# Causal masks of a differential attention moved off TensorE, with narrow diagonal tiles paired and the projections paced by each tile's surplus of ScalarE time

## The reference, cut to what matters

```python
xn = rmsnorm(x, norm_mix_g); u = xn @ w_in          # b, c, v_a | q, k, v | gates
y_a = short_gated_conv(b_g, c_g, v_a, conv_w) @ w_a_out
# four heads, each with two softmax maps of width 64 (c = 0, 1), values of width 128
s = einsum('bqhcd,bkhcd->bhcqk', q, k) * 64**-0.5
s = where(dist >= 0, s - slope[h] * dist, -inf)     # dist = qpos - kpos
p = softmax(s); a = p[:, :, 0] - lam * p[:, :, 1]
o = rmsnorm(einsum('bhqk,bkhv->bqhv', a, v), subln_g) * (1 - lam_init)
x = x + (g_a * y_a + g_b * (o @ w_b_out)) @ w_o     # sigmoid gates
x = x + square(relu(rmsnorm(x, norm_mlp_g) @ w_mlp_in)) @ w_mlp_out
out = rmsnorm(x, norm_final_g)                      # x: 4 x 4096 x 1024 float32
```

## Time and profile before

| | before |
|---|---|
| runs, us | 1248.42, 1382.58, 1246.85 (median 1248.42) |
| profiled execution, us | 1246.68 |
| its span, slowest core (3) | 1245.1 |
| spans of the eight cores | 1238.4 to 1245.1 |
| TensorE matmul busy | 1190.1 (96%) |
| VectorE busy | 596.2 (48%) |
| ScalarE busy | 643.8 (52%) |
| GpSimd busy | 62.1 (5%) |

### The profile page before, as it was taken

The page is one execution under the profiler, slowest core; times in us unless marked ns, Lnnn a source line. Parts: engine busy times, 40 slices in busy tenths (PEclk is TensorE's granted clock), DMA queues, the critical chain, the costliest instruction groups (busy, mean ns, idle before and its releaser), DMA issues.

```text
span 1245.1 us, 27807 instructions; the slowest of 8 cores (1238.4 to 1245.1 us)
## 1 busy us (share of the span) xinstructions
PE 1190.1 (96%) x7688; PEld 591.8 (48%) x7688; DVE 596.2 (48%) x964; ACT 643.8 (52%) x1010; POOL 62.1 (5%) x78
## 2 busy tenths in 40 slices
PE   3799999999999999999999999999999999999994
PEld 1355455555555555554444444444444444444442
DVE  3566426353434434323346436427364554637765
ACT  3455347888877897777755774330302112030066
POOL 0000001000000000000000000000000000000024
PEclk9899999999999999999999999999999999999998
DMA  8567310000100000018740507010321303031024
GB/s 169 154 179 185 75 35 2 2 3 2 36 2 3 2 2 3 2 36 150 186 104 1 135 2 131 23 34 1 68 32 38 68 1 68 1 69 21 14 86 186
DMA packets 17192, 71.97 MB, mean 58 GB/s; under 512 B 2416, under 2 KB 2672, under 8 KB 14608
## 3 DMA queue, kind: packets, MB, share of 16 engines
q0 software_dynamic: 6768, 35.65, 16.8%
q1 hardware_dynamic: 10272, 34.55, 8.0%
HBM read 97.46 MB, written 8.39 MB: 85 GB/s over the span
## 4 chain that ended last, share of the span: by engine, by line
PE 91%; DMA 2%; DVE 2%; ACT 2%; issue 1%; POOL 0%; DVEq 0%; ACTq 0%; POOLq 0%; SPq 0%
PE ps_all L294 71%; PE ps_all L291 11%; PE ps_all L296 7%; PE ps_all L315 1%; DMA big<-xs 1%; DMA big<-w_in 1%; ACT big L302 1%; DVE big L609 0%; ACT big L575 0%; DVE big L1089 0%; DVE big L318 0%; PE ps_all L641 0%; DVE big L1071 0%; ACT big L1084 0%; ACT big L304 0%
## 5 line engine op out<-in xcount | busy, mean ns | idle before, releaser
L294 PE MATMUL ps_all<-big 128*128 128x512 bf16 (+2 forms) x4416 | 950.0, 369 | 18.1 <-DVE big L318 14.9
L294 PEld LDWEIGHTS ps_all<-big 128*128 128x128 bf16 x4416 | 406.2, 98 | 500.7 <-issue 54.6
L575 ACT ACTIVATE big<-ps_all,big 128x512 bf16<-128x512 f32 (+3 forms) x384 | 313.8, 866 | 68.3 <-PE ps_all L296 26.9
L1059 ACT ACTIVATE big<-ps_all 128x512 bf16<-128x512 f32 x128 | 76.4, 597 | 336.6 <-PE ps_all L294 336.2
L1071 DVE TENSOR_TENSOR big<-ps_all,big 128x512 f32<-128x512 f32 x256 | 176.3, 691 | 39.2 <-PE ps_all L294 35.4
L291 PE MATMUL ps_all<-big 128*128 128x129 bf16 x2176 | 165.5, 221 | 3.2 <-DVE big L609 1.1
L291 PEld LDWEIGHTS ps_all<-big 128*128 128x128 bf16 x2176 | 129.3, 98 | 43.1 <-issue 35.7
L1060 DVE TENSOR_TENSOR big<-big 128x512 bf16<-128x512 bf16 x128 | 54.6, 426 | 165.9 <-ACT big L1059 165.9
L296 PE MATMUL ps_all<-big 64*128 64x512 bf16 (+3 forms) x640 | 114.6, 354 | 2.3 <-ACT big L575 1.1
L302 ACT ACTIVATE big<-big 128x1024 bf16<-128x1024 f32 (+1 forms) x65 | 68.6, 1055 | 60.0 <-PE ps_all L294 25.5
L318 DVE TENSOR_TENSOR big<-ps_all,big 128x1024 bf16<-128x1024 bf16 (+1 forms) x49 | 59.0, 1205 | 40.3 <-PE ps_all L315 40.3
(11 more groups left out here) (57 smaller groups left out, 387.7 us busy)
## 6 DMA issues: line engine op xcount, KB each, us to landing
big<-xs SPq DMA_DIRECT2D x48, 512.0 KB, 6.3
big<-w POOLq DMA_DIRECT2D x16, 1024.0 KB, 12.4
big<-w_g POOLq DMA_DIRECT2D x16, 512.0 KB, 7.6
out<-big SPq DMA_DIRECT2D x16, 512.0 KB, 3.0
big<-w_in POOLq DMA_DIRECT2D x12, 512.0 KB, 7.3
big<-w_o POOLq DMA_DIRECT2D x1, 2048.0 KB, 23.0
big<-w_a POOLq DMA_DIRECT2D x1, 1024.0 KB, 8.4
big<-w_b POOLq DMA_DIRECT2D x1, 1024.0 KB, 8.2
```

The costliest lines, as they stand in the source:

```text
L294: S.op("pe", lambda e: e.matmul(out, lhsT, rhs, start=start, stop=stop), reads=reads, writes=writes)
L575: S.op("act", lambda e, a=a, b=b, bi=bi: e.activation(PT[:, :, a:b], Sps[:, buf, :, a:b], AF.Exp, bias=btab[:, bi:bi + 1], scale=0.125), r ...
L1059: S.op("act", lambda e: e.activation(r, ph, AF.Relu), reads=[phk], writes=[rk])
```

## The change

- The mask matmuls, `tri` and `omask` and their loads go. Diagonal tiles of kind 0 get an `affine_select` on GpSimd, in place on the first 128 columns of `PT` (both maps, 128x256), which writes 0 where the key lies behind the query. For kind 1 the masked 128 columns become a piece of their own in the exponential, with a bias from 20 new columns of `btab` that contain -30000 on cores of even parity.
- The diagonal tiles with `cs` 256, and those with `cs` 384, of both kinds share a step: their scores lie side by side in the same PSUM buffer, their exponentials and value matmuls follow each other. 320 steps become 288.
- `cum` sums `spare(st)`: the exponentials' time beyond that of the step's matmuls, and 0.3 for a head's first step. `SPAN` is its value 24 steps before the end.
- The planner takes a selected tile as ready 0.9 us after its exponential.

```diff
             tiles = []
-            for c in range(4):
-                tiles += [(0, 4 * i + c, 128 * c, True), (1, 4 * i + c, 128 * c, True)]
+            for c in range(2):
+                tiles += [[(0, 4 * i + c, 128 * c, 0, True)], [(1, 4 * i + c, 128 * c, 0, True)]]
+            for c in range(2, 4):
+                tiles.append([(0, 4 * i + c, 128 * c, 0, True), (1, 4 * i + c, 128 * c, 512 - 128 * c, True)])
             for cc in range(4 * i):
-                tiles += [(0, cc, 0, False), (1, cc, 0, False)]
+                tiles += [[(0, cc, 0, 0, False)], [(1, cc, 0, 0, False)]]
...
-        if st["diag"]:
-            mask, mkey = (tri, "tri") if st["kind"] == 0 else (omask, "omask")
+        for kind, cc, cs, off, diag in st["subs"]:
+            kt = 16 * kind + cc
             for m in range(2):
-                mm(Sps[:, buf, m, cs:cs + 128], ident, mask, False, True, reads=["ident", mkey],
-                   writes=["pb%d" % (2 * buf + m)])
+                mm(Sps[:, buf, m, off:off + 512 - cs], KT[64 * m:64 * m + 64, h, kt * 128:(kt + 1) * 128],
+                   QT[64 * m:64 * m + 64, h, i * 512 + cs:(i + 1) * 512], True, True,
+                   reads=["KT%d_%d" % (h, kt // 4), "qo%d_%d" % (i, h)], writes=["pb%d" % (2 * buf + m)], tp=(64 * m, 0))
+
+    def exp_pieces(st):
+        out = []
+        for kind, cc, cs, off, diag in st["subs"]:
+            b0 = (kind * 16 + cc - 4 * st["i"] + 12) * 5
+            cuts = []
+            if diag and kind == 1:
+                cuts.append((cs, cs + 128, 160 + 5 * (cs // 128)))
+                rest = cs + 128
+            else:
+                rest = cs
+            if st["h"] == 0:
+                cuts = [(a, b, bb + a // 256) for a, b, bb in cuts]
+                cuts += [(max(rest, 256 * u), 256 * u + 256, b0 + u) for u in range(2) if max(rest, 256 * u) < 256 * u + 256]
+            else:
+                cuts = [(a, b, bb + 1 + st["h"]) for a, b, bb in cuts]
+                if rest < 512:
+                    cuts.append((rest, 512, b0 + 1 + st["h"]))
+            out += [(off + a - cs, off + b - cs, bi) for a, b, bi in cuts]
+        return out
...
+        for kind, cc, cs, off, diag in st["subs"]:
+            if diag and kind == 0:
+                blk = PT[:, :, off:off + 128]
+                S.op("pool", lambda e, blk=blk: e.affine_select(blk, blk, [[0, 2], [1, 128]], ALU.is_ge, 0.0,
+                                                               base=0, channel_multiplier=-1),
+                     reads=[ptkey], writes=[ptkey])
...
     def exp_cost(st):
-        w = 512 - st["cs"]
-        if st["h"] == 0 and w > 256:
-            return 0.57 + 2 * w * 0.00076
-        return 0.28 + 2 * w * 0.00076
+        return sum(0.28 + 2 * (b - a) * 0.00076 for a, b, bi in exp_pieces(st))
+
+    def spare(st):
+        return max(0.0, exp_cost(st) - 0.2 - st["width"] * (0.00042 + 0.056 / 64)) + (0.3 if st["first"] else 0.0)
 
     cum = [0.0]
     for st in steps:
-        cum.append(cum[-1] + exp_cost(st))
-    SPAN = cum[-1] - 24.0
+        cum.append(cum[-1] + spare(st))
+    SPAN = cum[-24]
...
-            r_pv = exp_end[pv_n] + LAT
+            r_pv = pt_ready[pv_n] + LAT
...
-            clk["pe"] += (512 - st["cs"]) * 0.00042
-            if st["diag"]:
-                set_mode(0)
-                clk["pe"] += 0.11
+            clk["pe"] += st["width"] * 0.00042
             emit_exp(qk_n)
             clk["act"] = max(clk["act"], clk["pe"] + LAT) + exp_cost(st)
             exp_end[qk_n] = clk["act"]
+            pt_ready[qk_n] = clk["act"] + (0.9 if st["subs"][0][4] and st["subs"][0][0] == 0 else 0.0)
```

More of the change, by code:

```diff
@@ L228, in build_program @@
     ident = pers.take([128, 128], BF16)
[L229 to L231 removed]
+    btab = pers.take([128, 180], F32)
     cst = pers.take([128, 48], F32)
@@ L527, in build_program @@
             tiles = []
-            for c in range(4):
-                tiles += [(0, 4 * i + c, 128 * c, True), (1, 4 * i + c, 128 * c, True)]
+            for c in range(2):
+                tiles += [[(0, 4 * i + c, 128 * c, 0, True)], [(1, 4 * i + c, 128 * c, 0, True)]]
+            for c in range(2, 4):
+                tiles.append([(0, 4 * i + c, 128 * c, 0, True), (1, 4 * i + c, 128 * c, 512 - 128 * c, True)])
             for cc in range(4 * i):
-                tiles += [(0, cc, 0, False), (1, cc, 0, False)]
-            for n, (kind, cc, cs, diag) in enumerate(tiles):
-                steps.append(dict(i=i, h=h, kind=kind, cc=cc, cs=cs, diag=diag, first=(n == 0),
-                                  last=(n == len(tiles) - 1), hid=hid, kt=16 * kind + cc))
+                tiles += [[(0, cc, 0, 0, False)], [(1, cc, 0, 0, False)]]
+            for n, subs in enumerate(tiles):
+                steps.append(dict(i=i, h=h, subs=subs, first=(n == 0), last=(n == len(tiles) - 1), hid=hid,
+                                  width=sum(512 - u[2] for u in subs)))
             hid += 1
@@ L567, in emit_exp @@
         pt_of[n] = (PT, ptkey)
[L568 to L577, removed]
+        for a, b, bi in exp_pieces(st):
+            S.op("act", lambda e, a=a, b=b, bi=bi: e.activation(PT[:, :, a:b], Sps[:, buf, :, a:b], AF.Exp,
+                                                                bias=btab[:, bi:bi + 1], scale=0.125),
+                 reads=["pb%d" % (2 * buf), "pb%d" % (2 * buf + 1), "btab"], writes=[ptkey])
@@ L582, in emit_pv @@
         PT, ptkey = pt_of[n]
         pv_done.add(n)
[L584 to L589, removed]
+        for u, (kind, cc, cs, off, diag) in enumerate(st["subs"]):
+            kt = 16 * kind + cc
+            for m in range(2):
+                for qc in range(cs // 128, 4):
+                    g = 4 * m + qc
+                    a = off + qc * 128 - cs
+                    mm(Ops[:, g // 3, g % 3, :], PT[:, m, a:a + 128], Vh[:, kt, h, 0:129],
+                       st["first"] and u == 0 and g % 3 == 0, st["last"] and u == len(st["subs"]) - 1,
+                       reads=["V%d" % kt, "Vones", ptkey], writes=["pb%d" % (4 + g // 3)], shared=True)
@@ L867, in build_program @@
             emit_pv(pv_n)
-            clk["pe"] += 0.056 * (512 - st["cs"]) / 64
+            clk["pe"] += 0.056 * st["width"] / 64
             if st["last"]:
@@ L1170, in _bias_table @@
                 tab[:, kind, r, 1 + h] = SLOPES[h] * (kpos - 512)
-    return tab.reshape(128, 160).astype(np.float32)
+    masked = tab[:, 1, 12:16] + (NEG if par == 0 else 0.0)
+    return np.concatenate([tab.reshape(128, 160), masked.reshape(128, 20)], axis=1).astype(np.float32)
 def make_in_maps(inputs):
@@ L1200, in make_in_maps @@
         "ident": np.eye(128, dtype=np.float32).astype(ml_dtypes.bfloat16),
-        "tri": np.where(np.arange(128)[:, None] > np.arange(128)[None, :], NEG, 0.0).astype(np.float32).astype(
-            ml_dtypes.bfloat16),
     }
@@ L1216, in make_in_maps @@
         m["btab"] = _bias_table(par)
-        m["omask"] = np.full((128, 128), NEG if par == 0 else 0.0, dtype=np.float32).astype(ml_dtypes.bfloat16)
         maps.append(m)
```

16 lines of the change are left out of this document (4 added, 12 removed).

## The result

After the change the kernel takes 1225.4 us (1224.54, 1225.66 and 1225.21), before it 1247.6 on the same chip (1248.42, 1246.85 and 1246.47; one disturbed execution of each, near 1380, is left aside). The ratio is 0.9829, with a 95% interval from 0.9813 to 0.9846: 22 us, or 1.7%, less. It is less than the 2% that the prediction takes a measurement to tell, but by its interval it is a gain. The forecast was 1226.

The account below looks back on a forecast made before the run. TensorE was taken to bound the attention, 371.1 of 382.5 us; -14.3 - 7.0 - 1.0 + 0.3 + 2.0 = -20.0 us from 1246.7 gave 1226.7, forecast as 1226 us, range 1217 to 1238.

Parts of the forecast that it names:

- Masks, -14.3: In the attention, 256 mask matmuls leave TensorE, the bounding engine, saving 14.3 us.
- Changes, 64 + adjacency: Tiling-mode changes on TensorE: 64 go with pairing, -7.0 us; score pairs meeting without masks between, 0 to 5 us, taken 1.
- Narrow pairs, +0.3: Two narrow score pairs following each other in a shared step lose 0 to 1.9 us, taken 0.3.
- Exponentials, +12 us of ScalarE at no cost: ScalarE's exponentials go from 384 to 428, +12.0 us busy, about 326, costing 0 while TensorE covers it.
- Selection, taken as 1.0 us: Each of 64 GpSimd selections takes 1.0 us (0.6 to 2.5); waits for selections and pows 0 to 12, taken 2.0.
- The first selection once late: Rival: the first selection's code must be fetched, 5 us once before the first value matmuls, 1232 us; chance 0.04.
- GpSimd's queue: Weight DMAs in GpSimd's queue have only a selection of 1 us ahead of them.
- Pacing, 0 (-3 to +3): Respreading the 480 projection matmuls in the attention gains nothing where TensorE bounds; 0 us, bounds -3 and +3.
- Outside the stage: The stretches ahead of and behind the attention would not move by more than 1 us.
- ScalarE as the bound: Rival: ScalarE's 326 us busy plus waits at heads and steps make 371 in the attention, 1235 us; chance 0.05.
- The slower case: Rival: selections take 2.5 us or more, a third covered by the lead, +48 us, 1294; chance 0.05.
- The larger gain: Rival: adjacent score pairs save 5 us, eviction waits lose 3 of 4.9, selections cost nothing; 1217 us, chance 0.18.

Follow-up runs that it names:

- R alone: The kernel before with only the new pacing (`spare` and its `SPAN`) added, masks and 320 steps kept; 1244.1 us.
- M with R: The kernel before with masks moved off TensorE and the new pacing, without pairing, 320 steps; 1229.2 us.
- the bias-piece kernel: The kernel after without the bias column and its own piece of the exponential, 384 exponentials instead of 428; 1227.0 us.

## Why the prediction was right, step by step

The time (1225.4 for 1226) and the stage (363.0 for 362.5) came out closer than their steps.

- **Masks, -14.3: right.** The group is gone, and R alone and M with R, which differ by the masks and by two changes, are 14.5 us apart in the stage. Work that is wholly on the bounding engine is the surest term of a sum.
- **Changes, 64 + adjacency: right in size, by luck in its parts.** Forecast -7.0 and -1.0 (about 570 changes), found 72 fewer, -7.8 (568). But the count is an outcome of the planner's order, not of the tiles: 552 with the masks alone, 492 with pairs, 568 with the pacing. The prediction took the old order as given and named 23 places at most where pairs could meet; with the old pacing 88 changes went with the masks alone.
- **Narrow pairs, +0.3: nothing.** In the kernel after two score pairs of 256 columns take 0.33 us to the next start (171.47 to 171.80) and two of 128 columns 0.22 (172.77 to 172.99), 0.325 and 0.218 in the middle of 16 each. What they stream and one change are 0.321 and 0.215.
- **Exponentials, +12 us of ScalarE at no cost: right.** 428 instructions, 325.3 us for 326; leaving them out gained nothing.
- **Selection, taken as 1.0 us: mis-sized, it took 0.42**, below even the lower bound of 0.6 from the earlier trace rows. Neither neighbour was a good one: the pow's 1,012 ns are for 4 elements, and the product is in float32 with two inputs. The waits of +2.0 for it and the pow behind it were 0.2; what the rest grew by, +2.5, came from waits for ScalarE (+1.3) and evictions (+0.6) and small ones. So the term was right in sum and wrong in cause.
- **The first selection once late: did not happen.** The first one stands with 0.41 us and nothing late behind it. The rule of the Trainium skill ("GPSIMD Engine Reference", 2.1 Instruction dispatch) of about 6 us at the first call of freshly loaded code shows nowhere for this instruction: either its code was there already, or it was paid where nothing shows, and the traces do not tell which.
- **GpSimd's queue: overlooked, at no cost in this order.** The prediction said of the weight loads only that a selection stands ahead of *them*. It did not ask what stands behind a load, nor what the program issues in front of it: some 99 waits for the pair of `w_g`, about 290 for `w_b`. That costs 6.7 us under the old pacing and 7.26 us of waiting in front of a pow. The row for it was there: in the trace of before the same pair of loads has a gap of 5.7 us in front of its row, with the same 99 waits, and no instruction of GpSimd stood behind it then.
- **Pacing, 0 (-3 to +3): right for the pacing alone (-2.5), wrong for its place in this change (-12.6).** The argument "where TensorE bounds, moving its work moves nothing" overlooks that without its masks TensorE runs up to a wait for ScalarE at the diagonal tiles when no projections stand among them (at the last head 5 to 6 us, above), and that the order of side work also decides the changes and where the loads are issued. A forecast of the change without this part by the same steps would have been 1226, and the kernel takes 1238.
- **Outside the stage**: behind it right (0.3 us). Ahead of it 4.4 us on core 3, more than the 1 us allowed; core 3 of before is the latest of cores that start over a spread of 6.7 us. What made it run at 0.97 there, and start late, was not tried.

Of the rivals, ScalarE as the bound is excluded by the bias-piece kernel. The slower case named the right quantity, but its price was nearly three times too high: at 2.55 us for a selection the stage is 25 us longer (0.39 us for each) where it had 69, which lands 6 us above before and not 47, because blocks 1 to 3 cover nine tenths of it. The larger gain asked for shorter eviction waits; they did not shrink (5.5 for 4.9).

## What to carry to other kernels

Price the work that leaves the bounding engine, then ask which order the scheduler will make of what is left: here two parts that each took work away made the kernel slower together (1230.4 to 1238.0) until the side work was spread anew. For every instruction put on GpSimd look at what is issued ahead of it there, waits included: a long list of waits shows in the trace only as a gap before the row of what follows, and it is the program's own. A helper that waits once for each reader of a region should wait for the last one only. A planner's price that looks too high may stand for a latency: change it only with the count of waits in view.

## What the runs showed of the hardware

- **Waits are instructions, and take time when they are met.** 94 in a row on GpSimd took 6.4 us, 0.06 to 0.07 each; 278 in front of `w_b` filled 17.5 us in the kernel after (508.9 to 526.4). Selections and pows behind them stand. The two loads of `w_g` themselves take 1.13 us.
- **Standing costs twice.** After waits of 4.93 and 7.26 us TensorE's matmuls came at twice their pitch for some microseconds (1.77 us for what takes 0.97), at the lower level of its two clocks (granted 0.50); in the kernel with the selection five times, 0.83 was granted between 200 and 240 us, among many waits of 1 to 2 us.
- **A change of tiling mode costs 0.108 us each way** at full clock. Thirty changes fewer were worth 2.9 us of the stage, at a price of 3.2. The Trainium skill ("TensorEngine Tiling (Array Packing)", Key Properties) says that a change of mode drains the engine; the rows agree and give it a size.
- **The affine selection** of 128x256 bf16 in place takes 0.41 us for the most part (mean 0.426 of 64), and five in a row, each on the result of the one before, 2.55, 0.51 each.
